# Another order of VectorE's and ScalarE's work in the token mixer, with four convolution buffers in place of two

## The reference

```python
def mixer(h, ...):
    proj = h @ w_in                     # q, k, v, z, beta, a, B, C, h_in
    qkv = silu(causal_dw_conv(qkv_ext, conv_gdn))     # four taps
    q, k = l2_normalize(q) * DK ** -0.5, l2_normalize(k)
    beta, g = sigmoid(b_raw), -exp(a_log) * softplus(a_raw + dt_bias)
    o, s = gdn_chunks(q, k, v, beta, g, s0, chunk)    # gated delta rule
    o = o * rsqrt(mean(o * o) + EPS) * gdn_norm * silu(z)
    y_sc = gate_b * causal_dw_conv(gate_c * h_in, conv_sc)   # three taps
    return concatenate([o, y_sc]) @ w_out

def trunk(x, ...):
    for l in range(DEPTH):              # DEPTH = 2
        x = x + 0.5 * rms_norm(swiglu(rms_norm(x, ng[0]), ...), ng[1])
        x = x + rms_norm(mixer(rms_norm(x, ng[2]), ...), ng[3])
        x = x + 0.5 * rms_norm(swiglu(rms_norm(x, ng[4]), ...), ng[5])
```

## Time and profile before

| what | us |
|---|---|
| median of 3 runs | 1516.93 (1515.77 to 1517.74) |
| profiled execution | 1521.55 |
| its span, first to last instruction | 1519.7 |
| TensorE busy in the span | 1458.1 (96%) |
| VectorE busy | 868.0 (57%) |
| ScalarE busy | 618.8 (41%) |
| GpSimd busy | 41.9 (3%) |

### The profile page before, as it was taken

How to read it: one execution, slowest core, us unless ns; L and a number is a source line. 1 busy time by engine, 2 the same in 40 slices (tenths; PEclk the granted TensorE clock), 3 DMA queues, 4 the chain that set the end, 5 groups by cost and what they waited for, 6 DMA issues and landing times.

```text
span 1519.7 us, 22795 instructions
## 1 busy us (share of the span) xinstructions
PE 1458.1 (96%) x9600; PEld 1418.2 (93%) x9600; DVE 868.0 (57%) x1453; ACT 618.8 (41%) x977; POOL 41.9 (3%) x132
## 2 busy tenths in 40 slices
PE   6999999999998999999999999999999999999996
PEld 5999999879987999999999999999799789999996
DVE  3655533877467675554376554347864766665533
ACT  4443333463322544433354433345433235434331
POOL 0000000110000000000000000010100000000001
PEclk9999999899999999999999999999999999999998
DMA  6444344122113344334454443442211143444342
GB/s 257 145 147 139 120 146 164 71 84 88 56 56 119 111 165 141 139 122 145 150 188 146 139 139 123 153 141 84 83 61 56 56 172 114 139 155 151 126 151 91
DMA packets 48612, 191.23 MB, mean 126 GB/s; under 512 B 6048, under 2 KB 7328, under 8 KB 47872
## 3 DMA queue, kind: packets, MB, share of 16 engines
q1 hardware_dynamic: 47520, 183.35, 35.1%
q0 software_dynamic: 992, 6.44, 1.0%
HBM read 183.33 MB, written 6.43 MB: 125 GB/s over the span
## 4 chain that ended last, share of the span: by engine, by line
PE 90%; DVE 5%; ACT 2%; issue 1%; DMA 1%; SPq 1%; POOL 0%; DVEq 0%; ACTq 0%; POOLq 0%
PE PS L1329 25%; PE PS L1331 24%; PE PS L1330 24%; PE PS L1482 5%; PE PS L1369 2%; PE PS L1374 2%; PE PS L1370 2%; PE PS L1480 1%; DVE CV L1068 1%; DVE WL L954 1%; PE PS L1645 1%; DMA RAW<-in_w_up 1%; PE PS L1515 1%; PE PS L1597 1%; ACT WH L704 0%
## 5 line engine op out<-in xcount | busy, mean ns | idle before, releaser
L1329 PE MATMUL PS<-XH,WH 128*128 128x336 f32 (+1 forms) x1728 | 556.6, 322 | 4.0 <-DVE WL L954 3.0
L1331 PE MATMUL PS<-XH,WL 128*128 128x336 f32 (+1 forms) x1728 | 545.6, 316 | 0.0
L1330 PE MATMUL PS<-XL,WH 128*128 128x336 f32 (+1 forms) x1728 | 545.4, 316 | 0.0
L954 DVE TENSOR_TENSOR WL<-RAW,WH 128x1024 fp32r<-128x1024 f32 (+1 forms) x312 | 398.4, 1300 | 200.9 <-ACT WH L704 200.9
L704 ACT ACTIVATE WH<-RAW 128x1024 fp32r<-128x1024 f32 (+1 forms) x312 | 343.9, 1118 | 207.8 <-DMA RAW<-in_w_down 171.6
L1329 PEld LDWEIGHTS PS<-XH,WH 128*128 128x128 f32 x1728 | 326.8, 189 | 23.9 <-issue 20.8
L1330 PEld LDWEIGHTS PS<-XL,WH 128*128 128x128 f32 x1728 | 327.3, 189 | 0.0
L1331 PEld LDWEIGHTS PS<-XH,WL 128*128 128x128 f32 x1728 | 326.8, 189 | 0.0
L1329 PE MATMUL PS<-HH,WH 128*128 128x336 f32 (+1 forms) x704 | 221.0, 314 | 0.0
L1331 PE MATMUL PS<-HH,WL 128*128 128x336 f32 (+1 forms) x704 | 220.4, 313 | 0.0
L1330 PE MATMUL PS<-HL,WH 128*128 128x336 f32 (+1 forms) x704 | 220.2, 313 | 0.0
(11 more groups left out here) (225 smaller groups left out, 1328.1 us busy)
## 6 DMA issues: line engine op xcount, KB each, us to landing
RAW<-in_w_up SPq DMA_DIRECT2D x176, 512.0 KB, 4.2
RAW<-in_w_down SPq DMA_DIRECT2D x64, 704.0 KB, 4.0
RAW<-in_w_in SPq DMA_DIRECT2D x56, 512.0 KB, 4.2
RAW<-in_w_out SPq DMA_DIRECT2D x16, 512.0 KB, 4.1
SEQ_S<-in_states SPq DMA_DIRECT2D x2, 2048.0 KB, 11.2
out_state_s<-SEQ_S POOLq DMA_DIRECT2D x2, 2048.0 KB, 6.9
...
```

Source lines behind the costliest of these rows:

```text
L954: dve.tensor_tensor(WL[slot][:, cols], RAW[slot][:, cols], WH[slot][:, cols].bitcast(F32), ALU.subtract).then_inc(split_lo.sem, 1)
L1329: pe.matmul(out, wh, xh, start=first, stop=False)
L1330: pe.matmul(out, wh, xl, start=False, stop=False)
L1331: return pe.matmul(out, wl, xh, start=False, stop=last)
```

## The change

1. The gate's sums are read by VectorE in a step of its own, `gate_read`, behind tiles 0 and 1. Convolution 0 goes ahead of `gate_cols`; convolutions 2 and 3 and their taps go ahead, between the blocks `gb`, and four Silu follow one another. `conv_at` puts the later convolutions elsewhere.
2. q, k and v use four buffers CV. CV2 and CV3 lie in the memory of VS, which is written later.
3. At the mixer's entry ScalarE takes all squares of X ahead of the split, and VectorE their sum ahead of two low parts (`x_sum`). TensorE takes `x_columns` after the first step of `gate_rows`, `x_rows_out` after the fourth.
4. ScalarE loads the table of the exponential right behind the logarithm.
5. `rob`, `o_inv` and `o_low` go behind the work of their slot (`BEHIND`), and of chunk 13's `hi` and `lo`, which were in `finish`, three go into the last slots and one behind XL.
6. In the FFNs `x_columns` goes behind the seventh step of chunk 2 and `x_rows_out` behind the eleventh.

```diff
+BEHIND = ("rob", "o_inv", "o_low")
...
-    steps = [("entry",), ("gate_rows",), ("evac", 0), ("evac", 1), ("tap", 0), ("tap", 1)]
+    steps = [("entry",), ("gate_rows",), ("evac", 0), ("evac", 1), ("gate_read",), ("tap", 0), ("tap", 1)]
     slot_work = [[] for _ in range(end)]
-    slot_work[0] += [("gate_cols",), ("evac", 2), ("evac", 3), ("hi", 1, 0), ("conv", 0), ("hi", 1, 1)]
-    slot_work[1] += [("gate_g",), ("lo", 1, 0), ("conv", 1)]
-    slot_work[2] += [("lo", 1, 1)]
-    slot_work[3] += [("cum",)]
-    slot_work[4] += [("gb", ORDER[0])]
-    slot_work[5] += [("gb", ORDER[1]), ("gb", ORDER[2])]
-    slot_work[6] += [("silu", 0), ("tap", 2), ("conv", 2), ("silu", 1), ("tap", 3)]
-    slot_work[7] += [("sq", 0), ("conv", 3), ("sq", 1)]
-    slot_work[8] += [("silu", 2)]
-    slot_work[9] += [("silu", 3)]
+    slot_work[0] += [("conv", 0), ("gate_cols",), ("evac", 2), ("tap", 2), ("evac", 3), ("tap", 3), ("hi", 1, 0), ("hi", 1, 1)]
+    slot_work[1] += [("gate_g",), ("conv", 1)]
+    slot_work[2] += [("lo", 1, 0)]
+    slot_work[3] += [("cum",), ("lo", 1, 1), ("conv", 2)]
+    slot_work[4] += [("gb", ORDER[0]), ("conv", 3)]
+    slot_work[5] += [("gb", ORDER[1]), ("gb", ORDER[2]), ("silu", 0)]
+    slot_work[6] += [("silu", 1), ("silu", 2), ("silu", 3)]
+    slot_work[7] += [("sq", 0), ("sq", 1)]
...
-    conv_at = {n: max(9 + (7 * (n - 4)) // 3, (tile[n] - first) * PARTS + 4) for n in range(4, QKV_T)}
+    conv_at = {n: max(7 + 2 * (n - 4), (tile[n] - first) * PARTS + 4) for n in range(4, QKV_T)}
...
+    slot_work[end - 3].append(("hi", N_IN - 1, 0))
+    slot_work[end - 2] += [("lo", N_IN - 1, 0), ("hi", N_IN - 1, 1)]
...
-        steps += sum(fillers[:1], []) + slot_work[now] + sum(fillers[1:], [])
+        ahead = [work for work in fillers[:1] if work[0][0] not in BEHIND]
+        steps += sum(ahead, []) + slot_work[now] + sum(fillers[len(ahead):], [])
...
-        CV = [CV0, CV1]
+        (CV2, CV3), cv_end = stack(g_at, ("CV2", [P, G_LEN], F32), ("CV3", [P, G_LEN], F32))
+        CV = [CV0, CV1, CV2, CV3]
...
                 for m in range(KT):
                     x_high(layer, j, m)
-                    if m < 4:
+                    if m < 4 or j == 1:
                         x_square(layer, j, m)
                     elif m < 6:
                         split_high(layer, third, m - 4)
-                for m in range(4, KT):
-                    x_square(layer, j, m)
+                if j == 1:
+                    for half in range(2):
+                        split_high(layer, third, half)
+                else:
+                    for m in range(4, KT):
+                        x_square(layer, j, m)
...
-                    if n >= 2:
-                        act.wait_ge(act_out.sem, silu_of("qkv", n - 2, layer))
-                    act.activation(CV[n % 2][:, 0:G_LEN - 3], EXT[:, n, 0:G_LEN - 3], ACT.Copy,
+                    if n >= 4:
+                        act.wait_ge(act_out.sem, silu_of("qkv", n - 4, layer))
+                    act.activation(CV[n % 4][:, 0:G_LEN - 3], EXT[:, n, 0:G_LEN - 3], ACT.Copy,
...
                         act.activation(T3, T2, ACT.Ln, bias=1.0).then_inc(to_dve.sem, 1)
+                        act.preload_act_table(ACT.Exp)
...
                         tap0_of(layer, 2 * N_IN - 1)
-                        split_ahead(layer, AT_OUT - 1)
...
+                    if j == 0:
+                        x_sum(*nxt)
                     for half in range(2):
-                        split_low(nxt[0], FIRST_CHUNK[nxt[1]] + 2, half)
+                        split_low(nxt[0], third, half)
+                    if j > 0:
+                        x_sum(*nxt)
                     x_norm(*nxt)
...
                         convolve(layer, 2 * N_IN - 1)
-                        split_ahead(layer, AT_OUT - 1)
...
+                        split_low(*ahead(layer, AT_IN + N_IN - 1, 2), 1)
...
-                            if c == 2 and (half, kt) == (0, 3):
+                            if c == 2 and (half, kt) == (1, 2):
+                                x_rows_out(layer, j)
+                            if c == 2 and (half, kt) == (0, 6):
...
                                 x_columns(layer, j)
-                        if c == 2 and half == 0:
-                            x_rows_out(layer, j)
...
-                            if kt == 3:
+                            if kt == 0:
                                 x_columns(layer, 1)
+                            elif kt == 3:
+                                x_rows_out(layer, 1)
                         ins.then_inc(filled.sem, 1)
-                        x_rows_out(layer, 1)
```

16 lines of the change are left out of this document (10 added, 6 removed).

## The result

| | before | changed |
|---|---|---|
| median us (14 runs each) | 1517.42 (1514.24 to 1519.04) | 1520.21 (1518.18 to 1525.52) |
| profiled execution | 1521.55 | 1520.38 |
| its span | 1519.7 | 1518.5 |

The ratio changed to before is 1.0027, with a 95% interval from 1.0018 to 1.0035: 4.1 us slower, 2.7 to 5.3. It lies close to the ratio of the means (1521.0 and 1517.0), in which three runs near 1525 count; the medians of the table differ by 2.8. The forecast was +4.0 and 1520.9.

What follows compares the result with a forecast made beforehand. TensorE was taken to bound the kernel (90% of the chain), so order pays only at its waits and the low clock behind them. 2 x (3.7 - 2.9) + 2.4 = +4.0 us gave 1520.9, range 1518 to 1524.

Steps and rivals of the forecast that it cites:

- Part 1: Chain to the gate: SEQ_GB at 296.1, TensorE on 0.8 us sooner, low clock at 298.42 probably gone; worth nothing alone.
- Part 2: Mixer's start, SEQ_GB to tile 8: DA and SQX come later, tile 8 at 319.7; each start 3.7 us longer.
- the clock: Restart at tile 8 in the mixer's start: same clock loss as before, 1.5 us either way per layer for the range.
- Part 3: Mixer's end: waits for out_o 0 and out_o 2 go, 1.3 us left for XL; each end 2.9 us shorter.
- 11.9 us of waits: TensorE's waits over two layers that the change can touch: low halves of weights, first squares, gate's decays, BY.
- Part 4: FFNs: row product 1.4 us later, a wait of 0.6 us before chunk 3 in each of four, 2.4 us.
- The early load: Exponential table load behind the logarithm on ScalarE: takes 1.28 us, no drain, costs nothing that VectorE waits for.
- (a): Mixer's start breaks even, tile 8's WL out by 316.04: -3.4 us, 1513.5; chance 0.10.
- (c): No wait at chunk 3 in the FFNs, its WL comes in time: +1.6 us, 1518.5; chance 0.20.
- (d): Mixer's end gains nothing, XL held by UEXT of tile 27: +7.4 + 2.4, about 1526.7; chance 0.08.
- (b): Start's three TensorE waits and both low stretches vanish, squares at 309.7: -23 + 2.4, about 1496; chance 0.07.
- The sum: Whole kernel: starts, ends and FFNs together +4.0 us, 1525.6 for the profiled execution, 1520.9 for the median.

Runs made afterwards that it cites:

- da_first: The changed kernel with convolutions 2 and 3 behind all DA instructions on VectorE: 1514.92 us, ratio 0.9984 to the kernel before.
- lo_first: The changed kernel with the first WL for tile 8 ahead of convolution 4 on VectorE: 1517.76 us, ratio 1.0008 to the kernel before.
- start_only: The changed kernel with the old end of the mixer and the old places in the FFNs: 1525.14 us, ratio 1.0057 to the kernel before.
- no_preload: The changed kernel without the early load of the exponential's table: 1521.69 us, ratio 1.0034 to the kernel before.
- split_only: The kernel before with the last output chunk's split early and XL ahead of the last low half, normalisation unmoved: 1521.49 us, ratio 1.0031.
- early_squares: The changed kernel with old FFN places, convolutions 2 and 3 behind DA, SQX behind the second Silu, later convolutions in old slots: 1505.03 us, ratio 0.9920.

## Why the prediction was right, and where not

**Part 1** held. SEQ_GB was put at 296.1 and came at 294.84, which is 295.6 with the 0.76 us by which this mixer starts earlier; RB was 0.5 us sooner than forecast too (287.63, so 288.4, against 288.9). The low stretch at 298 went. That this is worth nothing by itself follows from the wait of 5.63 us behind it; no run has this part alone.

**Part 2** held in mechanism; its size was too small. The last DA group was put at 306.5 (305.15 + 0.76 = 305.9), SQX at 315.2 (314.7), tile 8 at 319.7 (319.2); the waits at "some 6" and 2.7 (5.63 and 2.72). da_first and lo_first confirm what it hangs on, the two convolutions ahead of DA and WL behind convolution 4. In waits and starts the term is 3.2 us, not 3.7, per layer. The runs of start_only give 4.3. The step that was mis-sized is the clock, "put at the same loss as before". Against the trace of before that holds at this place (5.30 us at low clock behind tile 8 instead of 6.27, and 0.4 of the 3.2 us come back until the solve). But that trace has the low clock at both places in both layers, which the other traces of the old start don't, and start_only and no_preload lose 1.6 us or more per layer again some 130 us further on. The 3.7 lies between the two, and the prediction had kept 1.5 us either way for it.

**Part 3** held to a tenth: 2.9 us per mixer forecast; 38.61 us instead of 41.52 from the delta rule's last wait to the first product with XL; 1.27 left for XL against 1.3. What the prediction did not see is that one of its two edits gives nothing, and that alone it costs (split_only). It had credited both. The wait of 1.45 us stands in the earlier trace rows as "issue" and is missing from the prediction's 11.9 us of waits; it went as forecast all the same.

**Part 4** held: the idle time is 0.47 us in an FFN, and chunk 3 starts 0.64 late, which is what the 0.6 stood for. The four add 2.3 us, 2.4 forecast. The row product comes 1.4 us later and 0.64 of that shows, so the slack was some 0.7 with the semaphore in it, 0.9 without; 1.84 us more of delay became 1.85 more of waiting. (The row that the prediction cites for 0.153 gives 3.76 / 24 = 0.157, with the slow first product in it; 0.153 is what the later ones take. Nothing hangs on it.)

**The early load** cost nothing, as the row had said.

**The rivals.** (a) needed tile 8 at 316.04, it came 3.2 us later. (c) needed no wait at chunk 3, four came. (d) needed XL held by UEXT, XL came early. (b) was not what this order does, but the reason I gave was too strong: "six us before ScalarE can have them" is true of the order as it stood; in early_squares ScalarE has the squares at 306.70, with the same instructions. I had taken a bound of the order for one of the engine's work.

**The sum.** +4.0 against +4.1 is luck to the tenth. The measured parts are 8.6, -5.8 and +2.3, where 7.4, -5.8 and +2.4 were forecast; they make 5.1, the whole change measured 4.1 with an interval from 2.7 to 5.3, and the medians differ by 2.8. That the kernel gets a few us slower, and where, is what held.

**The median against the trace.** The sum was made against a profiled execution and moved by 4.6 us to the median. That is safe only for parts that don't hang on what was unusual in that execution, and the clock at the mixer's start was (twelve starts, above). The same shows in early_squares: its trace is 16.6 us shorter than that of before, its median 12.1. The difference of the spans of before and the changed kernel, -1.2, has the wrong sign. Stage by stage the two traces give 2 x (2.8 - 2.9) + 4 x 0.64 = +2.4. Against that, 0.8 us lie at the very first product (12.93 us and 12.16), and some 1.9, an estimate from half of the busy time, in low stretches at the start of two FFNs (6.83 us at 516.87 and 1267.81, 3.41 at 518.33 and 1269.26 in the changed kernel), behind waits that the change leaves alone.
